# The first tile's expert gates scattered into DRAM by accumulating DMAs, the samples picked by quarters, gate stores from ScalarE's queue

## What is computed

```python
def block(xt):                                    # one tile of tokens
    q = jnp.einsum('td,dhq->thq', xt, w_pq)
    s1 = jnp.einsum('thc,kc->thk', q[..., :half], keys1)
    s2 = jnp.einsum('thc,kc->thk', q[..., half:], keys2)
    v1, i1 = lax.top_k(s1, 16)
    v2, i2 = lax.top_k(s2, 16)
    cand = (v1[..., :, None] + v2[..., None, :]).reshape(T, 8, 256)
    sc, ci = lax.top_k(cand, 16)
    eid = i1[ci // 16] * 128 + i2[ci % 16]
    gate = jax.nn.softmax(sc, -1)
    hid = jax.nn.gelu(jnp.einsum('td,thkd->thk', xt, expert_u[eid]))
    return jnp.einsum('thk,thkd->td', gate * hid, expert_v[eid])
```

## Time and profile before

| | us |
|---|---|
| median of 3 runs | 2104.66 (2099.07 to 2105.82) |
| the profiled execution | 2104.66, of it a span of 2102.9 |
| PE busy | 2014.8 (96%) |
| DVE busy | 1619.8 (77%) |
| ACT busy | 793.6 (38%) |
| POOL busy | 543.4 (26%) |

### The profile page before, as it was taken

The page is one execution under the profiler, slowest core; times in us unless marked ns, Lnnn a source line. Parts: engine busy times, 40 slices in busy tenths (PEclk is TensorE's granted clock), DMA queues, the critical chain, the costliest instruction groups (busy, mean ns, idle before and its releaser), DMA issues.

```text
span 2102.9 us, 33945 instructions
## 1 busy us (share of the span) xinstructions
PE 2014.8 (96%) x12943; PEld 1848.3 (88%) x12943; DVE 1619.8 (77%) x3030; ACT 793.6 (38%) x1311; POOL 543.4 (26%) x334
## 2 busy tenths in 40 slices
PE   8998889889999899999999999999989999999998
PEld 8998879768866899999999999999978888888886
DVE  6635766565254325999999799999969999999997
ACT  4335453442241322332344344444434333333332
POOL 0000020000000000112111045555537656666530
PEclk9999889999999999999999999999999999999999
DMA  5223210061451402677676579999999999999982
GB/s 172 85 98 117 81 52 1 23 224 41 177 193 54 161 1 97 223 271 253 221 246 241 182 240 333 330 333 331 336 377 388 411 412 411 411 412 411 408 353 92
DMA packets 205520, 483.75 MB, mean 230 GB/s; under 512 B 11983, under 2 KB 104655, under 8 KB 205286
## 3 DMA queue, kind: packets, MB, share of 16 engines
q1 hardware_dynamic: 159334, 314.56, 41.3%
q0 software_dynamic: 46080, 167.79, 21.6%
HBM read 423.29 MB, written 58.36 MB: 229 GB/s over the span
## 4 chain that ended last, share of the span: by engine, by line
PE 57%; DMA 2%; SPq 1%; ACT 0%; DVE 0%; issue 0%; POOL 0%; ACTq 0%; DVEq 0%
PE ps L3000 24%; PE ps L2608 8%; PE ps L2604 8%; PE ps L2603 8%; PE ps L2594 5%; PE ps L2632 3%; DMA experts<-peer_u 1%; DMA outputs<-peer_v,kept 1%; SPq L2585 1%; SPq L2563 0%; ACT scores L2689 0%; DMA hidden<-kept 0%; PE ps L3026 0%; ACT kept L2678 0%; SPq L2552 0%
## 5 line engine op out<-in xcount | busy, mean ns | idle before, releaser
L3000 PE MATMUL ps<-v_high_low,gated_high_low 128*128 128x512 f32 x2304 | 526.1, 390 | 9.2 <-ACT gated_high_low L3068 7.5
L3000 PEld LDWEIGHTS ps<-v_high_low,gated_high_low 128*128 128x128 f32 x2304 | 434.0, 188 | 101.1 <-ACT v_high_low L3066 7.8
L2603 PE MATMUL ps<-x_high_low,u_high_low 128*128 128x384 f32 x1024 | 355.6, 347 | 0.2 <-ACT u_high_low L2669 0.2
L2604 PE MATMUL ps<-x_high_low,u_high_low 128*128 128x384 f32 x1024 | 345.0, 337 | 0.0
L3092 POOL DMA_INDIRECT outputs<-peer_v,kept x138 | 258.3, 1871 | 154.9 <-DVE kept L3109 118.3
L2720 POOL DMA_INDIRECT scores<-peer_u,kept x64 | 94.1, 1470 | 733.7 <-DVE kept L2840 556.8
L2678 ACT ACTIVATE kept<-ps 128x384 f32<-128x384 f32 x128 | 62.9, 491 | 405.8 <-PE ps L2608 402.6
L2608 PE MATMUL ps<-x_high_low,u_high_low 128*128 128x384 f32 x1024 | 204.7, 341 | 0.0
L2603 PEld LDWEIGHTS ps<-x_high_low,u_high_low 128*128 128x128 f32 x1024 | 192.5, 188 | 0.5 <-ACT u_high_low L2669 0.5
L2604 PEld LDWEIGHTS ps<-x_high_low,u_high_low 128*128 128x128 f32 x1024 | 192.8, 188 | 0.0
L3109 DVE SCALAR_TENSOR_TENSOR kept<-outputs,kept 128x1024 f32<-128x1024 f32 x136 | 174.2, 1281 | 8.4 <-DMA outputs<-peer_v,kept 4.7
(11 more groups left out here) (471 smaller groups left out, 4123.5 us busy)
## 6 DMA issues: line engine op xcount, KB each, us to landing
experts<-peer_u SPq DMA_DIRECT2D x63, 1024.0 KB
raw_v<-peer_v SPq DMA_DIRECT2D x60, 1024.0 KB
hidden<-kept SPq DMA_DIRECT2D x64, 384.0 KB
gates<-scores SPq DMA_DIRECT2D x12, 2048.0 KB
first_hidden<-hidden SPq DMA_DIRECT2D x16, 768.0 KB, 10.2
outputs<-gates SPq DMA_DIRECT2D x16, 768.0 KB
outputs<-hidden SPq DMA_DIRECT2D x16, 768.0 KB
first_gates<-gates SPq DMA_DIRECT2D x15, 768.0 KB
```

Of the source, the lines that this page charges most:

```text
L2603: pe.matmul(o, utr[:, b, HI, k], xr[:, HI, k, 0:DN], start=(k == 0), stop=False)
L2604: pe.matmul(o, utr[:, b, HI, k], xr[:, LO, k, 0:DN], start=False, stop=False)
L3000: ins = pe.matmul(bank(c, 2 * t + h), gr[:, slot, x, DN * b + P * t:DN * b + P * t + P], vr[:, slot, y, D * b + 512 * h:D * b + 512 * h + ...
```

## The change

Three things, in the terms of the code:

1. *Tile 0.* Its gates are no longer built from one-hot products. In phase_delta POOL sets a buffer to zero, and four DMAs of SP write it over the part of the gates' DRAM tensor that belongs to the first four token groups; ACT waits for them at the start of its work on the output projection, where the buffer is used again. In phase_hidden tile 0 is picked first; ACT makes the exps (at q = 5), DVE divides them and works out for each of a token's 128 pairs its place in DRAM (`place_first`), and POOL issues 128 indirect DMAs (`add_gate`), each of which adds one value per partition (token) to its place. After each 16 of them (one head) it waits until all have landed, since two heads can name the same expert. Between the 16 adds of a head stand 12 fetches of rows. Tiles 1 and 2 keep the products: 8 token groups for 12, 32 octets for 48, and the gates' stage begins at q = 47 for 39. The order of the picks is 0, 4, 3, 1, 2. 122 dots instead of 59 stand ahead of the stage.
2. *Samples.* phase_scores lays the samples' scores out so that each quarter of the partitions holds two of the eight heads, and `pick` for tile 4 works on 4 groups instead of 16 and on 32 pairs instead of 128.
3. *Stores.* `store_gates` moves from SP to ACT, ahead of the first token copies of the next group. SP waits at the end of the phase until the last of them has landed.

```diff
@@ phase_delta
+            sp.wait_ge(zeros_set, 1)
+            for q in range(0, NK // 4, 8):
+                sp.dma_start(gate_quads(c)[:, q:q + 8, 0:4].rearrange("p q g x -> p q (g x)"), zeros).then_inc(c.gates_zeroed, 16)
...
+            pool.memset(zeros, 0.0).then_inc(zeros_set, 1)
@@ phase_hidden
+ADDED = P // TG
+NOH = NTG - ADDED
+DO = NOH * TG
-BEFORE = NQ - QT * NTG - 1
+BEFORE = NQ - QT * NOH - 1
-GATES_AT = 25
-DOT_EVERY, LOW_EVERY = 2.2, 4.7
-DOTS_BY = {4: 0, GT: 16, 0: 32, 1: 46, 2: 59}
+PICKS = (0, 4, GT, 1, 2)
+EXPS_AT = {0: 5, GT: 19}
+DOT_EVERY, LOW_EVERY = 1.9, 4.9
+DOTS_BY = {0: 0, 4: 0, GT: 28, 1: 56, 2: 84}
+BEFORE_GATES = 122
+FETCHED_FIRST, FETCHED_BETWEEN = 5, 12
@@ SP
-            store_gates(NTG - 1, (NTG - 1) % 2)
+            sp.wait_ge(gkept, NOH * QG)
             sp.dma_start(gates_first[:, NTG - 1], gst[1][:, 0:4]).then_inc(c.first_gated, 16)
             store(NQ - 1, 1)
+            sp.wait_ge(gates_stored[1], 16 * (NOH // 2))
@@ ACT
+            def store_gates(tg, slot):
+                act.wait_ge(gkept, tg * QG + QG)
+                act.dma_start(gate_quads(c)[:, :, bass.ds(tg + ADDED, 1)]...).then_inc(gates_stored[slot], 16)
...
+            def exps_set(n):
+                act.wait_ge(picked, order[n] + 1)
+                act.activation(gates_of[n], kept[:, n, 2, 0:pairs_of(n)], ACT.Exp).then_inc(exp_s, 1)
+            span(act, 3, EXPS_AT[0], both)
+            exps_set(0)
+            span(act, EXPS_AT[0], EXPS_AT[GT], both)
+            exps_set(4)
+            exps_set(GT)
@@ POOL
+            def add_gate(i):
+                pool.indirect_dma_start(out=all_gates, out_offset=bass.IndirectOffsetOnAxis(ap=spot[:, i:i + 1], axis=0),
+                                        in_=gates_of[0][:, i:i + 1], in_offset=None, compute_op=ALU.add).then_inc(added, 16)
+            no = 0
+            while no < FETCHED_FIRST:
+                fetch(no)
+                no += 1
+            pool.wait_ge(spots_set, 1)
+            for i in range(PAIRS):
+                if i and i % TOPK == 0:
+                    pool.wait_ge(added, 16 * i)
+                add_gate(i)
+                while no < FETCHED_FIRST + FETCHED_BETWEEN * (i + 1) // TOPK:
+                    fetch(no)
+                    no += 1
+            while no < ROWSETS:
+                fetch(no)
+                no += 1
@@ DVE
+            def place_first():
+                divided(0)
+                key, quad = kept[:, 0, 0], spot
+                step(v.tensor_copy(quad, key))
+                step(v.tensor_scalar(quad, quad, 2, None, ALU.logical_shift_right))
+                step(v.tensor_copy(at_row, quad))
+                step(v.tensor_scalar(at_row, at_row, float(4 * DN - 4 * TG), token, ALU.mult, ALU.add))
+                step(v.scalar_tensor_tensor(at_row, key, float(TG), at_row, ALU.mult, ALU.add))
+                step(v.scalar_tensor_tensor(at_row, kept[:, 0, 1], float(NK * DN), at_row, ALU.mult, ALU.add))
+                v.tensor_copy(spot, at_row).then_inc(spots_set, 1)
```

More of the change, by code:

```diff
@@ L2725, in _ @@
             step = c.dve_step.on(v)
-            lows, dots, spent = [0], [0], [0.0, 0.0]
+            lows, dots, spent, due = [0], [0], [0.0, 0.0], []
             def low():
@@ L2735, in low @@
                 lows[0] += 1
+                if due and lows[0] >= UG * EXPS_AT[0] + 2:
+                    due.pop()
+                    place_first()
             def dot():
@@ new lines, in pick @@
+                v.tensor_tensor(few[:, :, 0:16], b2[:, 0, :, 0:1].broadcast_to([P, heads, 16]), b2[:, 1], ALU.add)
+                v.tensor_tensor(c3[:, :, 2:9], over(b2[:, 0, :, 1:8], 3, [P, heads, 7, 8]), over(b2[:, 1, :, 0:8], 2, [P, heads, 7, 8]), ALU.add)
+                step(v.tensor_tensor(c3[:, :, 9], b2[:, 0, :, 8:16], b2[:, 1, :, 0:1].broadcast_to([P, heads, 8]), ALU.add))
+                between(1.8 * part, upto)
+                t3, p3 = (x.rearrange("p (h k) -> p h k", k=TOPK) for x in (top, pair))
@@ L2836, in _ @@
-            v.wait_ge(picked, 1)
-            step(v.scalar_tensor_tensor(eid, kept[:, 4, 0], float(NK), kept[:, 4, 1], ALU.mult, ALU.add))
-            for i in range(QUADS):
-                r = slice(SAMP * i, SAMP * i + SAMP)
-                ins = v.tensor_copy(ids[r, 0:PAIRS_EACH], eid[r, PAIRS_EACH * i:PAIRS_EACH * i + PAIRS_EACH])
-            ins.then_inc(ids_set, 1)
-            v.wait_ge(xs_in, 16 * QUADS)
-            pick(GT, DOTS_BY[GT]).then_inc(picked, 1)
-            v.wait_ge(picked, 2)
@@ L2845, in _ @@
-            step(v.scalar_tensor_tensor(tail, kept[:, GT, 0], float(NK), kept[:, GT, 1], ALU.mult, ALU.add))
-            v.tensor_copy(ids[:, PAIRS_EACH:], tail).then_inc(ids_set, 1)
-            for n in range(3):
-                pick(n, DOTS_BY[n]).then_inc(picked, 1)
-                v.wait_ge(picked, n + 3)
-                if n == 1:
-                    while lows[0] < UG * GATES_AT + 1 and lows[0] < UG * BEFORE - 1:
-                        low()
-                    step(divided(4, 0))
-                    step(divided(GT, 1))
@@ L2855, in _, with expert_ids @@
-            while lows[0] < UG * BEFORE:
+                    between(cost * part, upto)
+                v.tensor_tensor(kept[:, n, 0:2, 0:r], spots[:, :, :, 0], spots[:, :, :, 1], ALU.add).then_inc(picked, 1)
+                v.wait_ge(picked, order[n] + 1)
+            def expert_ids(n, cols):
+                at = at_row[:, 0:pairs_of(n)]
+                step(v.scalar_tensor_tensor(at, kept[:, n, 0, 0:pairs_of(n)], float(NK), kept[:, n, 1, 0:pairs_of(n)], ALU.mult, ALU.add))
+                v.tensor_copy(ids[:, cols], at).then_inc(ids_set, 1)
@@ L2856, in _ @@
+            more, start = UG * BEFORE - lows[0], dots[0]
+            for i in range(more):
                 low()
+                while dots[0] < start + (BEFORE_GATES - start) * (i + 1) // more:
+                    dot()
+            divided(4)
+            divided(GT)
             v.wait_ge(sums, 1)
-            step(v.reciprocal(inv, bank(c, 6, DN)))
+            step(v.reciprocal(inv, bank(c, 6, DO)))
             v.tensor_tensor(kt[:, 3], gate, inv, ALU.mult).then_inc(gates_set, 1)
@@ L2862, in _ @@
             low()
-            before, octets = dots[0], NTG * QG // 2 + 3
-            for o in range(NTG * QG // 2):
+            before, octets = dots[0], NOH * QG // 2 + 3
+            for o in range(NOH * QG // 2):
                 t0, slot = OCT * o, o % 2
```

184 lines of the change are left out of this document (105 added, 79 removed).

## The result

The changed kernel takes **2150.24 us** (median of 4 runs, 2140.05 to 2152.1), the kernel before 2103.46 in the same job: ratio 1.0225, 95% interval [1.0206, 1.0243]. The change makes it 2.2% **slower**; I had forecast 2084 us, and 2115 as the upper end. The profiled execution has a span of 2149.1 us.

What follows compares the result with a forecast made beforehand. PE was taken to bound the kernel, so PE work removed counted as gained: -28.7 - 0.8 - 1.4 + 1 + 0 + 5 + 4 = -20.9 us from 2104.66 gives 2084 us, range 2074 to 2115.

Steps and rivals of the forecast that it cites:

- PE work removed: Search: with no one-hot products for the first tile, sixteen expert rows fall from 6.867 to 5.073 us, -28.7 us.
- Turn of pairs and sums: Turn of the picked pairs: three transposes and a wait go, sums run over 256 columns instead of 384, together -0.8 us.
- Loads of rows: PE's two waits for expert-row loads queued behind a gate store on SP go with the store on another queue, -1.4 us.
- End of the phase: SP's last hidden store leaves earlier, but SP waits for the last gate store to land: +1 us, between -2 and +3.5.
- Zeroing: POOL's memset and four 2 MB DMAs in phase_delta, where DMA is little used, cost 0; 36 us without that cover.
- rival 3: ACT is blocked by its own gate stores, eight times, costing 55 us: 2139 us; chance 0.03.
- DVE at the samples' pick: Around low 14 and the first dot, DVE brings lows late and PE waits: +5 us, bounds +3 and +7.
- POOL, +4: Eight blocks of 16 adds and 12 fetches, adds priced as fetches, take 45.9 us each: +4 us, bounds 0 and +11.
- the allowance: Time allowed for each of POOL's eight blocks before dot 100 is due at low 86: 356 / 8 = 44.5 us.
- rival 1: An add holds POOL longer than a fetch, each 0.1 us costing 12.8 us: 2129 us at 0.35 us more; chance 0.16.
- rival 2: The DMA engines are full, lacking 0.6 us per add, half of 75 us showing: 2103 us; chance 0.13.
- Dots held up by adds: Dots wait in half of the 128 adds by half of 0.94 us, 30 us: 2114 us; chance 0.02.

Runs made afterwards that it cites:

- late_adds: Changed kernel with 17 fetches instead of 12 per 16 adds in POOL's order and 106 dots instead of 122 ahead of the gates: 2085.74 us, ratio 0.9921.
- tuned_sp: tuned with the eight stores of gates put back from ScalarE's code (ACT) into SyncE's (SP), at their old places: 2087.62 us, ratio 0.9934.
- no_adds: Changed kernel without its 128 scattered adds and the waits for them, the first tile's gates missing from the output: 2078.01 us, ratio 0.9902.
- half_adds: Changed kernel with only every second scattered add (64 of 128), half of the first tile's gates missing: 2086.72 us, one run.
- tuned: late_adds with 19 fetches per 16 adds, 112 dots ahead of the gates, the first dot moved back, dots beside the one-hots ended four octets earlier: 2083.43 us.

## Why the prediction was wrong, by its own steps

- **PE work removed, -28.7**: held. The step is 6.867 us in the same 32 rows, and the rest 5.073 wherever nothing waits.
- **Turn of pairs and sums, -0.8**: held or better; the rows around it have 1.1 us over 5.073 a row in all in late_adds (rows 92 and 93), 3.0 before (rows 76 to 78).
- **Loads of rows, -1.4**: those waits are gone, but tuned_sp has none either with the stores on SP. Their cause, the queue, isn't shown. These three terms are -30.9 together; in late_adds the search is 18.6 us shorter than before although it loses 11.8 up to row 16, so they came to -30.4.
- **End of the phase, +1**: from the last third product to the combination's first product it was 9.1 us (1553.49 to 1562.6), now 6.9 (1604.20 to 1611.06). At -2.2 it is at the lower bound. The new wait is real, though: it cost 7 us in late_adds.
- **Zeroing, 0**: nothing speaks against it. The search begins at 816.62 instead of 819.91; it began between 814.2 and 822.0 in the experiments, and in that spread of 8 us no cost is visible. No run left the zeroing out.
- **ACT's store, rival 3**: each took 0.55 to 0.68 us of ACT's queue, and PE's step beside them stayed 6.867. Falls.
- **DVE at the samples' pick, +5 (bounds 3 and 7)**: the place and the mechanism were right, the size was 11.2. Two things were mis-sized. The first fetch stood at 886.92 and its dot began at 893.69, 6.8 us later, while I had taken 4.36; and the clock had no term. Why this row took longer to land stays open: the DMA engines were 0.99 busy in that stretch (below), but 0.92 around the first row before (871 to 876 us), which took 4.36. The changed kernel's timeline, POOL, DVE and PE:

```profile
886.92 1.11 POOL L2755 DMA_INDIRECT scores<-peer_u,kept  x1 [574.34 <-DVE kept L2936]
...
893.69 1.23 DVE L2800 SCALAR_TENSOR_TENSOR scores<-scores,experts 128x1024 f32<-128x1024 f32 x1 [6.34 <-DMA scores<-peer_u,kept]
...
895.62 1.21 DVE L2789 TENSOR_TENSOR u_high_low<-ps,u_high_low 128x1024 fp32r<-128x1024 f32 x1
...
896.88 2.93 PE L2631 MATMUL ps<-x_high_low,u_high_low 128*128 128x384 f32 x8 [6.64 <-DVE u_high_low L2789]
```

The dot waits for its row, the low behind it ends at 896.83, PE starts 0.05 us later. Its eight products then take 2.93 us where they take 1.57 in other rows. The windows give the granted clock (the last but two numbers):

```profile
886.00:890.00 4.00, 4.00 (x28) 3.89 (x26) 1.25 (x6) 3.34 (x4) 2.47 (x3) 1.00 0.38 114
890.00:897.00 7.00, 0.36 (x3) 0.12 (x1) 3.31 (x9) 0.73 (x1) 5.62 (x5) 0.81 0.99 390
897.00:901.00 4.00, 4.00 (x15) 3.90 (x16) 4.00 (x11) 0.49 (x1) 3.55 (x2) 0.50 0.96 278
```

PE stood idle for 6.6 us and then ran at 0.50, the 1.2 GHz level, for 4 us. Of the 11.2 us, 8.4 are waits (0.4, 1.4, 6.6), 2.8 this tail. Over rows 11 to 93 the excess is 79.6 us and the waits are 56 (56.6 less 0.5 in row 0): every 10 us of waiting cost some 4 more, 23.6 us in all. The granted clock agrees: 0.97 over 366 us and 0.90 over 114 us, for 1.00 before, make 22 us, an estimate from the windows shown above.

- **POOL, +4 (bounds 0 and 11): the step that failed.** It took an add at a fetch's price, 1.245 us from start to start, because it "addresses as many partitions"; an add took 1.88. Rows 16 to 93 lost 68.4 us, and the entry to the gates 4.7 more than in no_adds. By its own terms a block is 16 x 1.88 + 12 x 1.30 = 45.7, a landing wait of 2.1 (14.8 / 7) for 4.4, and by difference 5.7 for the lock (6.6 forecast): 53.5 for 45.9. The add alone makes +10.2. Over the allowance that is 9.0 us a block, 72 in eight, and 72 is what the adds cost by the runs (2150.2 - 2078.0). That the two agree to the microsecond is luck, since 44.5 was an estimate, but the size is right. So the bookkeeping held, and so did the threshold that it gave (from 0.17 us more per add the change is lost; it was 0.64 more). That is rival 1: its 12.8 us for each 0.1 us makes 81 us, and its chance of 0.16 was too low. The nearest row alone can't be both the price and the bound of an operation that the trace doesn't show: the range held 2115 where 0.64 us more gave 2150.
- **DMA engines full, rival 2**: up to the last add rows landed 5.3 us after issue in the median (4.2 to 8.5), adds 5.0, and half_adds and late_adds lost nothing in rows 16 to 76 with their 64 and 128 adds. Falls.
- **Dots held up by adds (the forecast's 0.02)**: of 160 dots the longest took 1.27 us. The other way it is true: POOL's add waits for DVE. The changed kernel's timeline of DVE and POOL:

```profile
982.78 4.42 DVE L2876 TENSOR_TENSOR experts<-experts,kept 128x4096 bf16<-128x4096 f32 x1
984.27 4.36 POOL L2760 DMA_INDIRECT gates<-gates_high,experts  x1 [0.30 <-issue]
987.24 1.23 DVE L2800 SCALAR_TENSOR_TENSOR kept<-kept,experts 128x1024 f32<-128x1024 f32 x1
```

The add ends 1.43 us after the one-hots do. The Trainium skill, SBUF — State Buffer (Who interferes with whom), says that a VectorE instruction with two SBUF inputs and a GpSimd instruction that reads SBUF exclude each other. The trace agrees where POOL comes second. It doesn't where an add comes first: 57 of the 160 dots began while an add ran, and none of these took longer than 1.23 us.

Without POOL's term the sum of the prediction was -24.9 us; without POOL's adds the kernel gained 23.1 by the medians (2101.15 to 2078.01), and 28.3 by the profiled spans (2102.9 to 2074.6). That is closer than its parts, so in part luck: +6.2 at the first dot stands against -4.7 behind the search and -5.7 ahead of it (it begins at 814.19 for 819.91), for neither of which a run shows a cause.

## What to carry to other kernels

Work taken off the bounding engine is worth nothing if its replacement goes through an engine that feeds it by rate. Before such a move, compare per block what the feeding engine needs with what the consumer allows, and give an operation that no row shows a range of prices above the nearest row (here the add took 1.5 times a fetch, start to start); if the sum stands at the limit already, spread the operation over a later stretch with room, as two numbers did here. Put a wait for a DMA's landing where the traffic around it is low (the late fetches cost 7 us here), and count for PE's waits the slow clock behind them.

## What the runs showed of the hardware

- A scatter of 128 elements from SBUF to DRAM holds POOL 0.98 us and makes 32 packets; one that adds holds it 1.58 us and makes 144 (start to start 1.28 and 1.88 us).
- After a wait of 6.6 us PE ran 4 us at a granted clock of 0.50; after one of 1.4 us (row 13) the products took 1.68 us for 1.57, no such tail.
- A store of 2 MB of gates landed 9 to 19 us after its issue from ACT's queue (no_adds, after, late_adds and tuned); all engines waited for the last one until 10.7 us after its issue in no_adds and tuned, and 17.3 in late_adds, where rows were gathered up to it.
- Beside the one-hots an add took 2.58 us in the median (25 adds of late_adds, 1320 to 1435 us), as fetches there take 1.68 instead of 0.94: POOL's price of either differs with what DVE runs beside it.
